# Gate and up projections with two input parts in one matmul, and a PSUM layout to match

## The chip, the cores and the metric

The kernel runs on one core of a Trainium2 chip. The metric is the device time of one execution in microseconds (us). TensorE (PE) multiplies, VectorE (DVE) and ScalarE (ACT) work elementwise, GpSimd (POOL) subtracts, SyncE (SP) starts the loads of weights. PSUM is the memory that matmuls write; one bank holds 512 fp32 values per partition.

## The reference, cut to what matters

The program is two transformer stacks in a row on 256 tokens of 1,024 features: two layers of (feed-forward, mixer of four branches, feed-forward), then four layers of (mixer, cross attention, feed-forward). The change is in the eight feed-forward stages:

```python
def _swiglu(x, w_gate, w_up, w_down):
    return (jax.nn.silu(x @ w_gate) * (x @ w_up)) @ w_down
# in each layer, D = 1024, D_FF = 2816 everywhere:
x = x + 0.5 * _swiglu(_rmsnorm(x, norm), w_gate, w_up, w_down)   # first stack
x = x + _swiglu(rmsnorm(x, norm), w_gate, w_up, w_down)          # second stack
```

## The kernel before

All weights are cut into 460 units of 1 MB (128 partitions x 2,048 fp32 values), used in a fixed order. Five slots hold them (`RING = 5`). For each unit SP loads `raw` once the unit five places earlier is done (L382 to L386), ACT makes the high part `wh` by rounding to the short fp32r form (L1113), and POOL makes the low part `wl = raw - wh` (L400). POOL takes over from unit 2; DVE makes the low parts of the first two (L1768, L1800).

Activations are kept features by tokens, also as a high and a low part (`ah`, `al` for the input of a stage, `gh`, `gl` for the gated values). A product of a weight tile of 128x128 with 256 tokens is three matmuls into the same 256 columns of a bank, each with its own load of the stationary tile (`product`, L451 to L457):

```python
pe.matmul(out, sl, vh, ...)   # L454  low weights  x high input
pe.matmul(out, sh, vl, ...)   # L455  high weights x low input
pe.matmul(out, sh, vh, ...)   # L456  high weights x high input
```

A unit is 16 such products, 48 matmuls of 256 columns. A feed-forward stage (`ffn`) has 22 units of gate and up in turn (0 gate, 1 up, 2 gate, and so on), each 2x256 columns in one bank of the ring G0 to G3, and then 11 units of `down` that accumulate in the four banks of S0 and S1. So gate and up are 176 units in the program, 2,816 products, 8,448 of the 24,180 matmuls.

The norm's factor per token (`root`, used through the view `along`) is not applied to the input but to the result in PSUM. It is ready only after unit 1, since the row sums are matmuls put halfway into and behind unit 1 (`row_sums_apart`, L560). For each pair of units DVE does five operations of 128x512 (`pair`, L1914 to L1929): scale the gate (L1919), scale the up value (L1921), multiply with ACT's silu (L1924), round to `gh` (L1927), subtract to `gl` (L1929). ACT does the silu between the first two and the third (L1269), and in its program order each silu stands behind the rounding of the unit four places ahead. PE takes a bank of G again when silu (for a gate unit) or the subtraction (for an up unit) four units earlier has passed.

Around a feed-forward stage stands this order. Its input arrives in PSUM: in the four G banks after a mixer, in S0 and S1 after another feed-forward stage, which happens once (end of layer 0 to begin of layer 1 in the first stack). DVE adds the residual (L1872, L1959), cuts the low part (L1776) and copies the sum to SBUF (L1783, signal `x_kept`); only then is the PSUM tile free.

In the first feed-forward stage the kernel also makes position tables: PE computes them behind unit 2 (L1077), DVE copies them (L1936), and ACT starts 12 DMAs (`send_tables`, L1683), one after each pair 1 to 8 and two after pairs 9 and 10. DVE waits for all 12 before the first mixer (L2753).

Of the kernel before, what the change touches and what calls it, by code (L numbers as in the profile page):

```python
# [128 lines left out]
def build(nc, w_units, params_d, consts_d, hot_d, rel_d, x_d, mem_d, ws_d, bs_d, out_d,  # L129
# [14 lines left out]
    wl = sb("wl", RING * UW, F32R, offset=at[0] - 4 * RING * UW)  # L144
    wh = sb("wh", RING * UW, F32R)
# [3 lines left out]
    ah = sb("ah", KD * T, F32R)  # L149
    al = sb("al", KD * T, F32R)  # L150
    full = sb("full", KD * T)
    mh = sb("mh", KD * T, F32R)
    ml = sb("ml", KD * T, F32R)
# [18 lines left out]
    gh = w("gh", 0, FP * 512, F32R)  # L172
    gl = w("gl", FP * 512, FP * 512, F32R)
# [17 lines left out]
    oh, ol = w("oh", 0, 2048, F32R), w("ol", 2048, 2048, F32R)  # L191
# [17 lines left out]
    hoh, hol = w("hoh", 4096, 2048, F32R), w("hol", 8192, 2048, F32R)  # L209
# [6 lines left out]
    soh, sol = w("soh", 8192, 2048, F32R), w("sol", 10240, 2048, F32R)  # L216
# [18 lines left out]
    G = [nc.alloc_psum_tensor(f"G{i}", [P, 512], F32) for i in range(4)]  # L235
    S = [nc.alloc_psum_tensor(f"S{i}", [P, 1024], F32) for i in range(2)]
# [126 lines left out]
    with nc.Block() as block:  # L363
# [49 lines left out]
        def _(pe):  # L413
# [4 lines left out]
            gfree, sfree = {}, {}  # L418
            also = {}

            def bank(ring, nxt, free, by, signals=1):

                k = nxt[0]
                nxt[0] += 1
                if k - len(ring) in free:
                    pe.wait_ge(*free[k - len(ring)])
                expect[by.name] = expect.get(by.name, 0) + signals
                free[k] = (by, expect[by.name])
                return ring[k % len(ring)]

            def g_bank(by):
                return bank(G, gbank, gfree, by)

            def s_bank(by, signals=1):
                if sbank[0] - len(S) in also:
                    pe.wait_ge(*also[sbank[0] - len(S)])
                return bank(S, sbank, sfree, by, signals)

            def g_bank_until(by, count):

                k = gbank[0]
                gbank[0] += 1
                if k - len(G) in gfree:
                    pe.wait_ge(*gfree[k - len(G)])
                gfree[k] = (by, count)
                return G[k % len(G)]

# [3 lines left out]
            def product(out, parts, start, stop, **kw):  # L451

                for k, (sh, sl, vh, vl) in enumerate(parts):
# [5 lines left out]
            def features(out, j, xh, xl, fcs=2, col=256, halfway=None):  # L459

                for fc in range(fcs):
                    if fc and halfway is not None:
                        halfway()
                    for k in range(KD):
                        parts = [(wcut(wh, j, k * 256 + fc * P, P), wcut(wl, j, k * 256 + fc * P, P),
                                  xh[:, k * T:(k + 1) * T], xl[:, k * T:(k + 1) * T])]
# [3 lines left out]
            def features_by_input(out, j, xh, xl, acts, pieces=False):  # L470

                for k in range(KD):
# [4 lines left out]
                    for fc in range(2):  # L477
                        parts = [(wcut(wh, j, k * 256 + fc * P, P), wcut(wl, j, k * 256 + fc * P, P),
                                  xh[:, k * T:(k + 1) * T], xl[:, k * T:(k + 1) * T])]
# [4 lines left out]
            def tokens_by_input(out, j, xh, xl, acts):  # L484

                for k in range(KD):
                    if k % 2 == 0:
                        pe.wait_ge(acts, c.next(acts))
                    for tb in range(TB):
                        a = k * T + tb * P  # L490
                        parts = [(xh[:, a:a + P], xl[:, a:a + P], wcut(wh, j, k * 256, 256), wcut(wl, j, k * 256, 256))]
# [4 lines left out]
            def tokens(out, j, xh, xl, first=0, width=256, base=0):  # L496

                for tb in range(TB):
                    parts = [(xh[:, k * T + tb * P:k * T + tb * P + P], xl[:, k * T + tb * P:k * T + tb * P + P],
                              wcut(wh, j, k * 256 + first, width), wcut(wl, j, k * 256 + first, width))  # L500
                             for k in range(KD)]
# [3 lines left out]
            def projection(count, by, xh, xl, acts=None, kind="features"):  # L505
                for u in range(count):
# [4 lines left out]
                    if kind == "features" and first is not None:  # L511
                        ins = features_by_input(out, j, xh, xl, first)
                    elif kind == "features":
                        ins = features(out, j, xh, xl)
                    elif first is not None:
                        ins = tokens_by_input(out, j, xh, xl, first)
                    else:
                        ins = tokens(out, j, xh, xl)
                    ins.then_inc(unit_done, 1)
                    unit[0] += 1  # L520

# [53 lines left out]
            def ffn(memory=False):  # L575
# [3 lines left out]
                g0 = gbank[0]  # L579

                def unit_of(j, u, n, free):
                    if free is not None:
                        pe.wait_ge(*free)
                    if n:
                        pe.wait_ge(low_ready, n + 1)
                    if u == 1:
                        part = row_sums_apart()
                    if u == 0:
                        ins = features_by_input(G[g0 % 4], n0 % RING, ah, al, acts_ready, pieces=n == 0)
                    else:  # L590
                        halfway = (lambda: part(0)) if u == 1 else None
                        if memory and u == 13:
                            sums = norm_sums_apart(memn)
                            halfway = lambda: sums(0, KD // 2)
                        ins = features(G[(g0 + j) % 4], (n0 + j) % RING, ah, al, halfway=halfway)
# [2305 lines left out]
```

## Time and profile before

| what | value |
|---|---|
| median of 3 runs | 2871.94 us |
| lowest and highest run | 2865.34 and 2881.08 us |
| profiled execution, first to last instruction (span) | 2878.8 us |
| PE busy | 2822.3 us, 98% |
| POOL, ACT, DVE busy | 73%, 46%, 37% |
| granted TensorE clock, mean | 0.989 |

The profile gives the profiled execution's span; no time of its own is listed beside it. It lies inside the three runs, 0.24% above their median. Durations of single matmuls (some 280 ns) contain the length of the pipeline; how fast matmuls follow each other is seen from the time of many divided by their number.

### The profile page before, as it was taken

How to read it: one execution, taken by the hardware profiler on the slowest of the kernel's cores; microseconds unless marked ns; L12 is line 12 of the kernel's file. 1: busy time of each engine (PE TensorE's matmuls, PEld its weight loads, DVE VectorE, ACT ScalarE, POOL GpSimd, SP SyncE). 2: the span in 40 equal slices, each digit the busy share in tenths (PEclk: the TensorE clock that was granted, in tenths of full speed). 3: DMA queues.
4: the chain of work that ended last, by engine and by line, in shares of the span. 5: the costliest groups of instructions: out<-in, count | busy, mean ns of one | idle time of the engine just before them, and what ended most of it. 6: DMA issues, size and time to landing. Idle time of an engine off the chain costs nothing.

```text
span 2878.8 us, 55910 instructions
## 1 busy us (share of the span) xinstructions
PE 2822.3 (98%) x24180; PEld 2771.7 (96%) x24180; DVE 1066.5 (37%) x1865; ACT 1333.4 (46%) x1490; POOL 2108.9 (73%) x462
## 2 busy tenths in 40 slices
PE   8999999999999999999999999999999999999998
PEld 8999889999999899999999998999999999999998
DVE  4217534213155443445333144333123331453331
ACT  5335544344355454345443484444354443454442
POOL 6777657878876578776768783659886688767785
PEclk9999999999999899999999999999999999999999
DMA  7974344555554355554445542445554455544553
GB/s 231 193 198 170 135 144 176 191 185 188 199 184 152 112 192 189 182 185 147 168 169 191 191 177 87 158 144 197 191 204 153 147 195 196 191 147 161 176 192 116
DMA packets 74197, 496.88 MB, mean 173 GB/s; under 512 B 8399, under 2 KB 13135, under 8 KB 14968
## 3 DMA queue, kind: packets, MB, share of 16 engines
q1 hardware_dynamic: 68344, 485.88, 46.9%
q10 hardware_dynamic: 5632, 7.62, 2.7%
q8 instruction: 191, 3.13, 0.4%
q14 instruction: 30, 0.25, 0.0%
HBM read 490.05 MB, written 3.41 MB: 171 GB/s over the span
## 4 chain that ended last, share of the span: by engine, by line
PE 86%; POOL 4%; DMA 3%; issue 3%; DVE 2%; ACT 2%; ACTq 0%; SPq 0%; POOLq 0%; DVEq 0%
PE G L454 21%; PE G L456 21%; PE G L455 21%; PE S L454 5%; PE S L456 5%; PE S L455 5%; POOL wl L400 4%; DMA raw<-w_units 2%; PE G L691 1%; PE S L1042 1%; ACT wh L1113 1%; DMA bias<-tables 0%; PE S L842 0%; PE S L799 0%; PE S L805 0%
## 5 line engine op out<-in xcount | busy, mean ns | idle before, releaser
L400 POOL TENSOR_TENSOR wl<-raw,wh 128x2048 fp32r<-128x2048 f32 x458 | 2108.7, 4616 | 740.5 <-ACT wh L1113 719.0
L1113 ACT ACTIVATE wh<-raw 128x2048 fp32r<-128x2048 f32 x456 | 873.7, 1918 | 1045.6 <-DMA raw<-w_units 1045.5
L454 PE MATMUL G<-ah,wl 128*128 128x256 f32 x4304 | 1209.2, 281 | 15.6 <-DVE wl L1768 8.9
L455 PE MATMUL G<-al,wh 128*128 128x256 f32 x4304 | 1200.6, 279 | 0.0
L456 PE MATMUL G<-ah,wh 128*128 128x256 f32 x4304 | 1200.3, 279 | 0.0
L454 PEld LDWEIGHTS G<-ah,wl 128*128 128x128 f32 x4304 | 816.4, 190 | 24.1 <-issue 15.1
L455 PEld LDWEIGHTS G<-al,wh 128*128 128x128 f32 x4304 | 815.2, 189 | 0.6
L456 PEld LDWEIGHTS G<-ah,wh 128*128 128x128 f32 x4304 | 814.1, 189 | 0.0
L454 PE MATMUL S<-gh,wl 128*128 128x256 f32 x1408 | 391.4, 278 | 3.4 <-POOL wl L400 3.4
L455 PE MATMUL S<-gl,wh 128*128 128x256 f32 x1408 | 391.3, 278 | 0.0
L456 PE MATMUL S<-gh,wh 128*128 128x256 f32 x1408 | 391.2, 278 | 0.0
L454 PEld LDWEIGHTS S<-gh,wl 128*128 128x128 f32 x1408 | 265.0, 188 | 3.7 <-issue 3.7
L456 PEld LDWEIGHTS S<-gh,wh 128*128 128x128 f32 x1408 | 265.1, 188 | 0.0
L455 PEld LDWEIGHTS S<-gl,wh 128*128 128x128 f32 x1408 | 265.1, 188 | 0.0
L1921 DVE TENSOR_TENSOR G<-G,root 128x512 f32<-128x512 f32 x88 | 61.5, 698 | 361.3 <-PE G L456 361.3
L1959 DVE SCALAR_TENSOR_TENSOR S<-S,x 128x512 f32<-128x512 f32 x28 | 19.6, 700 | 367.1 <-PE S L456 365.9
L1919 DVE TENSOR_TENSOR G<-G,root 128x512 f32<-128x512 f32 x88 | 61.4, 698 | 184.4 <-PE G L456 184.1
L454 PE MATMUL G<-mh,wl 128*128 128x256 f32 x384 | 108.3, 282 | 3.3 <-DVE ml L2120 2.8
L454 PE MATMUL G<-wh,al 128*128 128x256 f32 x384 | 108.0, 281 | 0.8 <-DVE ll L2563 0.8
L455 PE MATMUL G<-wl,ah 128*128 128x256 f32 x384 | 107.2, 279 | 0.0
L456 PE MATMUL G<-wh,ah 128*128 128x256 f32 x384 | 107.1, 279 | 0.0
L456 PE MATMUL G<-mh,wh 128*128 128x256 f32 x384 | 106.9, 279 | 0.0
(371 smaller groups left out, 3786.3 us busy)
## 6 DMA issues: line engine op xcount, KB each, us to landing
raw<-w_units SPq DMA_DIRECT2D x459, 1024.0 KB, 4.8
bias<-tables ACTq DMA_DIRECT2D x24, 128.0 KB, 3.2
tables<-trow ACTq DMA_DIRECT2D x12, 192.0 KB, 9.0
con<-consts SPq DMA_DIRECT2D x1, 1056.0 KB, 16.8
x<-x_in SPq DMA_DIRECT2D x4, 256.0 KB, 5.8
raw<-w_units SPq DMA_DIRECT2D x4, 256.0 KB, 6.9
memx<-mem_in ACTq DMA_DIRECT2D x1, 1024.0 KB, 7.4
out<-full SPq DMA_DIRECT2D x4, 256.0 KB, 2.5
```

The costliest lines, as they stand in the source:

```text
L400: pool.tensor_tensor(wl[:, j * UW:(j + 1) * UW], raw[:, j * UW:(j + 1) * UW], wh[:, j * UW:(j + 1) * UW].bitcast(F32), ALU.subtract)\
L454: pe.matmul(out, sl, vh, start=start and k == 0, stop=False, **kw)
L455: pe.matmul(out, sh, vl, start=False, stop=False, **kw)
L456: ins = pe.matmul(out, sh, vh, start=False, stop=stop and k == len(parts) - 1, **kw)
L691: ins = pe.matmul(out, v_of(kc), pt[:, kc * 512 + n * P:kc * 512 + (n + 1) * P], start=kc == 0, stop=kc == nk // P - 1)
L1042: ins = pe.matmul(out[:, h * T:(h + 1) * T], qf[:, f * T + g * P:f * T + (g + 1) * P], kc[:, f * T:(f + 1) * T], start=dc == 0, stop=dc == 1)
L1113: act.activation(wh[:, j * UW:(j + 1) * UW], raw[:, j * UW:(j + 1) * UW], ACT.Copy)\
L1919: dve.tensor_tensor(pairs(gate), pairs(gate), along, ALU.mult).then_inc(scaled, 1)
L1921: dve.tensor_tensor(pairs(value), pairs(value), along, ALU.mult).then_inc(up_scaled, 1)
L1959: dve.scalar_tensor_tensor(xs if last else held[k], held[k], factor, xs, ALU.mult, ALU.add)\
```

## The change

Three things change.

- Gate and up units use `slot_product`: a matmul with the high weights streams high and low input, 512 columns, into two slots of 256 in one bank, and a matmul with the low weights adds low weights x high input to the first slot. That is two matmuls and two loads for a product. The pairs of SBUF tensors become one tensor each, at the same addresses, so that one access pattern reaches both parts.
- A unit now fills two banks. Units take the four tiles of two banks (G01, G23, S0, S1) by a list, `unit_tiles`. Ordinary stages go round four tiles, starting with an S tile; the first stage and the one that also prepares the memory input go round three after unit 3.
- DVE scales both slots and adds them: three operations of 512 columns for each unit in place of one.

The tables move: their matmuls stand behind unit 5, the copy behind pair 2, and ACT starts two DMAs after each of the pairs 4 to 9. The residual units after a mixer start at an even G bank. All other products, the 88 `down` units among them, remain three matmuls.

```diff
+            def slot_product(bank, parts, start, stop):
+                two = bank.rearrange("p (s n) -> p s n", s=2)
+                for k, (sh, sl, vh, vl, both) in enumerate(parts):
+                    pe.matmul(two, sh, both, start=start and k == 0, stop=False, skip_group_check=True)
+                    ins = pe.matmul(two[:, 0, :], sl, vh, start=False, stop=stop and k == len(parts) - 1,
+                                    skip_group_check=True)
+                return ins
...
+            def slot_features(tile, j, xs, halfway=None):
+                for fc in range(2):
+                    if fc and halfway is not None:
+                        halfway()
+                    parts = [weights_still(j, k * 256 + fc * P, xs, k * T) for k in range(KD)]
+                    ins = slot_product(tile[:, fc * 512:(fc + 1) * 512], parts, True, True)
+                return ins
...
+    def unit_tiles(gbank, sbank, first, memory):
+        held, sums, other = [(gbank // 2 + n) % 2 for n in range(2)], 2 + sbank % 2, 2 + (sbank + 1) % 2
+        assert gbank % 2 == 0
+        if first or memory:
+            start = held + [other, sums] if first else [other] + held + [sums]
+            rest = [(held + [sums])[(u - 4) % 3] for u in range(4, 2 * FP - 1)]
+            return start + rest + held[0:1]
+        return [([other] + held + [sums])[u % 4] for u in range(2 * FP)]
...
# DVE, for each unit
+                def scale_slots(tile, spare):
+                    total, other = slots(tile)
+                    spare = pairs(full[:, spare * 512:(spare + 1) * 512])
+                    dve.tensor_tensor(spare, other, along, ALU.mult).then_inc(vec_step, c.one(vec_step))
+                    dve.tensor_tensor(total, total, along, ALU.mult).then_inc(vec_step, c.one(vec_step))
+                    dve.wait_ge(vec_step, c.sofar(vec_step))
+                    return total, dve.tensor_tensor(total, total, spare, ALU.add)
...
-                    dve.tensor_tensor(pairs(gate), pairs(gate), along, ALU.mult).then_inc(scaled, 1)
+                    scale_slots(Q[tiles[u - 1]], 2)[1].then_inc(scaled, 1)
...
# PE, for each unit u of tile t
+                    claim([2 * t, 2 * t + 1], (gated_ready, v0 + u // 2 + 1) if u % 2 else (silu_ready, s0 + u // 2 + 1))
...
# ACT
             def send_tables(p):
-                if p == 1:
+                if p == 4:
                     act.wait_ge(trow_ready, 2)
-                heads = {9: (8, 9), 10: (10, 11)}.get(p, (p - 1,)) if p else ()
+                heads = range(2 * p - 8, 2 * p - 6) if 4 <= p < 10 else ()
```

## Rows read from the trace of the kernel before

**Rows 1.** The page: busy time by engine, and the chain by engine.

```profile
PE 2822.3 (98%) x24180; PEld 2771.7 (96%) x24180; DVE 1066.5 (37%) x1865; ACT 1333.4 (46%) x1490; POOL 2108.9 (73%) x462
PE 86%; POOL 4%; DMA 3%; issue 3%; DVE 2%; ACT 2%; ACTq 0%; SPq 0%; POOLq 0%; DVEq 0%
```

**Rows 2.** Stretches (from:to length, busy time and count by engine, clock, DMA share, GB/s).

```profile
463.00:576.00 113.00, 113.00 (x960) 112.94 (x960) 38.64 (x56) 45.68 (x35) 92.32 (x21) 1.00 0.53 187
651.00:760.00 109.00, 109.00 (x962) 108.94 (x961) 38.64 (x56) 45.84 (x35) 93.34 (x21) 1.00 0.54 194
760.00:820.00 60.00, 60.00 (x532) 60.00 (x531) 7.26 (x13) 23.18 (x17) 51.22 (x12) 1.00 0.51 177
1141.00:1186.00 45.00, 45.00 (x382) 44.92 (x381) 26.22 (x36) 18.82 (x16) 34.29 (x8) 1.00 0.53 188
1187.00:1248.00 61.00, 61.00 (x521) 61.00 (x520) 8.32 (x14) 23.30 (x17) 49.95 (x12) 1.00 0.49 173
```

**Rows 3.** Pieces of the chain: start, length, what, count.

```profile
1412.63 6.91 PE S L1042 x32
```

**Rows 4.** Timeline of PE: start, length, what, count.

```profile
831.70 0.95 PE L549 MATMUL S<-ones,full 128*128 128x1 f32 x8
832.58 0.38 PE L725 MATMUL S<-x,sp 128*4 128x256 f32 x1
...
1475.75 0.59 PE L560 MATMUL S<-full,ones 128*128 128x256 f32 x2
1476.00 0.47 PE L454 MATMUL G<-ah,wl 128*128 128x256 f32 x1
1476.30 0.28 PE L455 MATMUL G<-al,wh 128*128 128x256 f32 x1
```

**Rows 5.** Groups by line: mean ns of one behind the busy time.

```profile
L400 POOL TENSOR_TENSOR wl<-raw,wh 128x2048 fp32r<-128x2048 f32 x458 | 2108.7, 4616 | 740.5 <-ACT wh L1113 719.0
L1921 DVE TENSOR_TENSOR G<-G,root 128x512 f32<-128x512 f32 x88 | 61.5, 698 | 361.3 <-PE G L456 361.3
```

**Rows 6.** Timeline of DVE, second and third stage with feed-forward.

```profile
467.54 0.70 DVE L1919 TENSOR_TENSOR G<-G,root 128x512 f32<-128x512 f32 x1
...
486.06 0.70 DVE L1921 TENSOR_TENSOR G<-G,root 128x512 f32<-128x512 f32 x1 [4.95 <-PE G L456]
...
641.11 1.28 DVE L1783 COPY x<-S 128x512 f32<-128x512 f32 x2
```

**Rows 7.** Timeline of PE where feed-forward follows feed-forward.

```profile
638.39 0.28 PE L456 MATMUL S<-gh,wh 128*128 128x256 f32 x1
638.50 0.28 PE L454 MATMUL G<-ah,wl 128*128 128x256 f32 x1
```

**Rows 8.** DMA from 50 to 200 us: queues (packets, MB, share), issues.

```profile
q1 hardware_dynamic: 3829, 27.86, 46.9%
q10 hardware_dynamic: 1584, 2.16, 38.0%
raw<-w_units SPq DMA_DIRECT2D x26, 1024.0 KB, 8.7
tables<-trow ACTq DMA_DIRECT2D x11, 192.0 KB, 9.0
```

**Rows 9.** First stage: stretches as in rows 2, and PE's wait.

```profile
100.00:140.00 40.00, 40.00 (x342) 40.00 (x341) 12.29 (x18) 14.86 (x10) 30.23 (x8) 1.00 0.93 218
140.00:180.00 40.00, 37.68 (x320) 37.50 (x320) 2.78 (x4) 13.89 (x8) 27.69 (x7) 1.00 0.94 212
PE S L454 <- POOL wl L400: 3.4, 2, 2.3
```

**Rows 10.** Timeline of ACT: arrivals of weights beside doubled tables.

```profile
149.99 1.31 ACTq L1683 DMA_DIRECT2D tables<-trow  x2
155.53 1.92 ACT L1113 ACTIVATE wh<-raw 128x2048 fp32r<-128x2048 f32 x1 [3.64 <-DMA raw<-w_units]
173.03 1.92 ACT L1113 ACTIVATE wh<-raw 128x2048 fp32r<-128x2048 f32 x1 [8.72 <-DMA raw<-w_units]
```

More of the change, by code:

```diff
@@ L417, in _, with claim, expected, g_bank_until @@
             expect = {}
[L418 to L426, printed above, removed]
-                expect[by.name] = expect.get(by.name, 0) + signals
-                free[k] = (by, expect[by.name])
-                return ring[k % len(ring)]
-            def g_bank(by):
[L432 to L446, printed above, removed]
+            busy = {}
+            def claim(banks, *until):
+                asked = []
+                for b in banks:
+                    asked += [w for w in busy.get(b, ()) if w not in asked]
+                    busy[b] = until
+                for w in asked:
+                    pe.wait_ge(*w)
+            def expected(by, signals=1):
+                expect[by.name] = expect.get(by.name, 0) + signals
+                return by, expect[by.name]
+            def g_bank_until(by, count):
+                b = gbank[0] % len(G)
+                gbank[0] += 1
+                claim([b], (by, count))
+                return G[b]
+            def g_bank(by):
+                return g_bank_until(*expected(by))
+            def s_bank(by, signals=1, *also):
+                k = sbank[0] % len(S)
+                sbank[0] += 1
+                claim([4 + 2 * k, 5 + 2 * k], expected(by, signals), *also)
+                return S[k]
+            inputs, memory, gated_in = (ahl, KD * T), (mhl, KD * T), (ghl, FP * 512)
+            heads, hgrn_heads, sgu_out = (ohl, KD * T), (hohl, 2 * KD * T), (sohl, KD * T)
             def wcut(t, j, first, width):
@@ L578, in ffn, with one @@
                 s0, v0 = expect.get("silu_ready", 0), c.taken.get("gated_ready", 0)
[L579 to L583, printed above, removed]
+                tiles = unit_tiles(gbank[0], sbank[0], n0 == 0, memory)
+                def one(u):
+                    n, t = n0 + u, tiles[u]
+                    claim([2 * t, 2 * t + 1], (gated_ready, v0 + u // 2 + 1) if u % 2 else (silu_ready, s0 + u // 2 + 1))
                     if n:
                         pe.wait_ge(low_ready, n + 1)
[L586 removed]
+                    if u == 0:
+                        ins = slot_features_by_input(Q[t], n % RING, inputs, acts_ready, pieces=n == 0)
+                    elif u == 1:
                         part = row_sums_apart()
[L588 to L595 removed]
+                        ins = slot_features(Q[t], n % RING, inputs, lambda: part(0))
+                    elif memory and u == 13:
+                        sums = norm_sums_apart(memn)
+                        ins = slot_features(Q[t], n % RING, inputs, lambda: sums(0, KD // 2))
+                    else:
+                        ins = slot_features(Q[t], n % RING, inputs)
                     ins.then_inc(unit_done, 1)
@@ L600, in unit_of @@
                         sums(KD // 2, KD)
+                        c.next(acts_ready, KD // 2)
+                    if n0 == 0 and u == 5:
+                        claim([6, 7], (trow_ready, 2))
+                        bias_tables()
                 for u in range(2 * FP):
-                    if u < 4:
-                        free = gfree.get(g0 + u - 4)
-                    else:
-                        free = (silu_ready, s0 + u // 2 - 1) if u % 2 == 0 else (gated_ready, v0 + u // 2 - 1)
-                    unit_of(u, u, n0 + u, free)
-                    if n0 == 0 and u == 2:
-                        bias_tables()
-                    if memory and u == 13:
-                        c.next(acts_ready, KD // 2)
+                    one(u)
                 unit[0] += 2 * FP
-                gbank[0] += 2 * FP
                 expect["silu_ready"] = s0 + FP
-                for k in range(4):
-                    u = 2 * FP - 4 + k
-                    gfree[gbank[0] - 4 + k] = ((silu_ready, s0 + u // 2 + 1) if u % 2 == 0
-                                               else (gated_ready, v0 + u // 2 + 1))
                 n1 = unit[0]
-                if not n0:
-                    pe.wait_ge(trow_ready, 2)
                 y = [s_bank(x_kept, 2), s_bank(x_kept, 2)]
```

211 lines of the change are left out of this document (116 added, 95 removed).

## The prediction

> **What bounds the kernel now.** I read the page first: busy time by engine and the chain by engine. PE is busy 98% of the span and is 86% of the chain; POOL is at 73%, DVE at 37% [rows 1]. So only what shortens PE's own stream pays, as long as nothing else becomes late. Then I read stretches, because the mean duration of a matmul (some 280 ns) is not its pace. In the gate and up part of the second feed-forward stage (463 to 576 us) 960 matmuls take 113.0 us, 117.7 ns each. In the third (651 to 760 us) 962 take 109.0 us, 113.3 ns each [rows 2]. The granted clock is 1.00 in both, the 2.4 GHz level, at which 256 columns are 106.7 ns. So a matmul of 256 columns costs 7 to 11 ns more than its columns, and there are two paces. They hold for long stretches and change between them: `down` runs at 112.8 ns in 760 to 820 us and at 117.1 in 1187 to 1248 us; the last gate and up units of the fourth stage (1141 to 1186 us) run at 117.8 [rows 2]. I call them quick and slow. The four last feed-forward stages read as the third. Counted over the program, some 62 of the 176 gate and up units are slow: 22 of the first stage, 22 of the second, 9 of the fourth, and the first one or two of the others, behind the row sums. 114 are quick.
>
> What makes the extra? Two kinds of rows. Eight matmuls of one column, each with a load of a 128x128 tile, start 0.88 us apart in all (831.70 to 832.58), 110 ns each [rows 4]: that is the price of a load with next to nothing to stream. And 32 matmuls of 256 columns in plain fp32 take 6.91 us, 216 ns each [rows 3]: they stream for 213 ns, and a load for each adds only 3. So a load of about 110 ns is hidden whole behind a stream of 213 ns, and is itself the limit, with a few ns of hand-over, behind one of 107 ns. That is what the change can win: of three loads for a product one goes, one hides behind 512 columns, and one still stands behind 256.
>
> **The product.** Before: 3 x 117.7 = 353 ns slow, 3 x 113.3 = 340 ns quick. After: the 512 columns at 216 ns, by the fp32 row that streams as long, and a 256-column matmul behind it. The nearest row for the second is the place where the stream goes from fp32 to fp32r: from the first of two sum matmuls at 1475.75 to L455 at 1476.30 are 0.55 us, less 2 x 0.216 leaves 118 ns for the L454 between [rows 4]. With the quick pace it would be 113. So 329 to 334 ns; I take 332, since the nearest row is on the slow side. The bounds: all loads hidden, columns alone, 768 at 2.4 GHz = 320 ns and two hand-overs of 3 ns make 326; and a cost that goes by columns, 3 x 113.3 = 340 ns.
> By 332: slow units 62 x 16 x 21 ns = 20.8 us, quick units 114 x 16 x 8 ns = 14.6 us. **Term 1: -35.4 us** (at 326 -52.3; at 340 -12.9).
>
> The trace shows a load at 110 ns and a matmul pace of 113 or 118 [rows 2, 4]. The Trainium skill, "TensorE: Matmul & The Clock Gate", section "Back-to-back issue gap", gives for a warm matmul N/2.4 + 2.5 ns, with the next load drawn ahead beside it. By that rule 256 columns cost 109.2 ns and a product 327.5 ns before and 325 after: the change would win 2.5 ns a product, 7 us in all. The trace speaks against its value for before (340 to 353) and agrees on the long stream (216 for 213); if its 325 held for after, term 1 would be about -55 us. The page's section "LDWEIGHTS (loading the stationary operand)" has 107 ns for 128 columns, and the row of one-column matmuls (110) is near it.
>
> **DVE and ACT.** Each unit gets two more operations of 128x512. The scaling took 698 ns [rows 5]; multiply to SBUF and add I put at the same. A pair then has 9 operations, 6.3 us and some waits, in a period of 2 x 16 x 0.332 = 10.6 us. DVE idles 4.95 us in front of the second scaling [rows 6], so there is room: it is hidden by PE's next unit. The gate's tile is free 2.1 + 0.6 us after its unit, the up tile 6 x 0.7 = 4.3 us after; with four tiles PE comes back three units later (15.9 us), with three tiles two units later (10.6 us). At the start of a stage the norm's factor comes late: the first scaling in the second stage begins at 467.54 [rows 6], when units 0 and 1 are done. Then silu is past at 470.3 and the up tile at 474; the first reuses come at about 473 and 478. Hidden. In the fourth stage unit 4 takes the tile of unit 1 (the list starts `other, G01, G23, sums` and goes on with G01), which is about 0 to 1 us late, once: 0.5 us. POOL needs 4.62 us for a unit [rows 5], PE will need 5.31: the supply still holds.
>
> **Where feed-forward follows feed-forward.** There the stage's input lies in S0 and S1, and unit 0 wrote to a free G bank: PE goes from `down` to unit 0 without a gap, 638.39 to 638.50 [rows 7]. After, unit 0 wants the S tile `other`, which is the second of these two. It is free when DVE's last copy to x has ended: 641.11 + 1.28 = 642.4 [rows 6], 3.9 us later. Nothing hides it, apart from 0.5 us that PE waits later for the row sums. **Term 2: +3.4 us**, once. After a mixer the S tile is free and the G banks are copied before unit 1: nothing.
>
> **The first stage and its tables.** Between 100 and 180 us the DMA engines are 93 and 94% busy [rows 9]. The tables hold 38.0% of 16 engines for 11 of them in 150 us, 5.2 us of all engines each; 26 units hold 46.9%, 2.7 us each [rows 8]. One table in each pair of units is 5.2 + 5.4 = 10.6 us of DMA in a pair of 11.3: it just fits. Two in a pair, as the change sends them from pair 4 to pair 9, are 15.8 us in a pair of 10.6. The trace shows what two do: after four tables at 137.7 and 150.0 ACT's next arrivals stand at 155.53, 162.39 and 173.03, with 8.72 us of idle time for the last [rows 10], and PE waits 3.4 us for POOL, in two waits [rows 9]. For twelve: the queue of tables lasts some 62/0.55 = 113 us from about 75 us on; the weights get 51 us of it, 19 units where PE wants 21. Two units are 11 us. Part of that the ring takes: with five slots the weights of a unit can be asked for four units early (21 us), of which landing (8.7 us [rows 8]), ACT and POOL (1.9 and 4.6) use 15, so 6 us are left. That makes a stall of 5 us, on top of one like the 3.4 us of now, which comes from the same cause; with the doubt in the sharing 3 to 12 us in place of 3.4. **Term 3: +5 us** (bounds -2, the early tables no longer delaying anything, and +20, if weights get only 40% of the DMA, as after 137.7 us). All tables land before some 190 us, ahead of the first mixer at 205: DVE's wait for them is hidden, but has only 15 us of cover.
>
> **The pace behind it.** `down` and the mixers are not touched, but pace is inherited from what ran before. If `down` turned quick in all three slow stages it would give 3 x 528 x 4.4 ns = 7 us, if slow in all five quick ones cost 11.6 us. I put nothing, and keep -7 and +12 for the range.
>
> **Sum.** -35.4 + 0.5 + 3.4 + 5 = -26.5 us on the span of 2878.8, which becomes 2852. The span is 0.24% above the median of the runs; the same step from 2871.9 gives **2845 us**, 0.9% less.
>
> **Rivals.**
> 1. Every load hides (326 ns). For it: the 216 ns of the fp32 rows, two passes with a load. Against: no 256-column fp32r stretch is under 113. Term 1 is -52.3, the time 2829. (The Trainium skill's rule above, from the section "Back-to-back issue gap", would end here too.)
> 2. Cost goes by columns, 340 ns: then the extra is in reading fp32r, not in the load. For it: quick pace and columns give the same ratio whatever is loaded. Against: the load at 110 ns alone. Term 1 is -12.9, the rest +9: 2868, no change to be seen.
> 3. Tables starve the first stage (+20 in place of +5): 2860. For it [rows 10]; against: the ring's lead had held with one table a pair.
> 4. Other side: the long stream leaves PE in the slow pace, and it lasts. Behind sums that stream 213 ns the pace was the slow one in the row I used. Of the matmuls outside gate and up 15,700 remain, some 8,200 of them now quick: 5 x 528 in `down` and, my estimate from the starts in the trace, 60% of the mixers' 9,400 fp32r ones. At 4.4 ns they cost 36 us, and the product 334, 5 us more: 2845 + 41 = 2886. It is slower than before from about 5,100 turned matmuls on. Against: the pace turned quick again within two units in six of the eight stages.
> 5. The change does not do what it says, if the DVE chain holds the tiles: it would show as waits on `gated_ready`; the 4.3 us against 10.6 leave it under 2 in 100, and I give it no case.
>
> **How the numbers follow.** Forecast 0.45 (its own range 2832 to 2857), rival 1 0.20, rival 2 0.16, rival 3 0.10, rival 4 0.09. What can be told from no change is 0.5%, 14 us: under 2857.6 is faster, over 2886.3 slower. Faster: 0.43 + 0.20 + 0.04 of rivals 2 and 3 = 0.67. Slower: rival 4 ends at the border; with mishaps beside it 0.07. Same: 0.26. The range goes from 2814 (rival 1 with quick `down`) to 2868, which cuts rival 4 and half of rival 2.
>
> **What would show it.** Between 1480 and 1590 us two matmuls take 332 ns together, and a unit 5.31 us in place of 5.44; 326 or 340 ns tell for rivals 1 and 2. At the one change from feed-forward to feed-forward PE's first wait is on DVE's copy, some 4 us. In the first stage PE waits for POOL between 120 and 190 us, 5 to 12 us in all. DVE's busy time grows by 176 x 2 x 0.7 = 246 us. Behind the last gate and up unit `down` stands at 113 or 118 ns. I am wrong if PE waits elsewhere in the gate and up units, or if a product is outside 326 to 340.

## The result and the profile after

The changed kernel takes 2931.04 us (median of 4 runs, 2928.02 to 2932.41), the kernel before 2875.26 us beside it (2865.34 to 2881.08). The ratio is 1.019, with a 95% interval of 1.017 to 1.022: it is slower by 56 us. I had forecast 2845 us and a range of 2814 to 2868, so even the sign is wrong. Of the two profiled executions the spans are 2929.0 and 2878.8 us, 50 us apart, at the same mean clock of 0.989.

The page of the changed kernel: busy time by engine, the groups of the slot products' two matmuls into the G tiles (L487 with 512 columns, L488 with 256; the S tiles have 1,280 more of each), and the landing time of the tables (issue count, KB, us):

```profile
span 2929.0 us, 50637 instructions
PE 2860.1 (98%) x21364; PEld 2678.1 (91%) x21364; DVE 1294.3 (44%) x2217; ACT 1339.2 (46%) x1490; POOL 2110.2 (72%) x462
...
L487 PE MATMUL G<-ahl,wlh 128*128 128x512 f32 x1536 | 555.8, 403 | 24.3 <-DVE wlh L1822 10.1
...
L488 PE MATMUL G<-ahl,wlh 128*128 128x256 f32 x1536 | 434.6, 283 | 0.0
...
tables<-trow ACTq DMA_DIRECT2D x12, 192.0 KB, 16.1
```

PE executes 2,816 matmuls fewer than in [rows 1] and is busy 38 us longer; it stays the bound. DVE gains 228 us of work and still has room. The timeline of PE in the second gate and up part (start, length, what):

```profile
520.10 0.28 PE L488 MATMUL G<-ahl,wlh 128*128 128x256 f32 x1
520.22 0.40 PE L487 MATMUL G<-ahl,wlh 128*128 128x512 f32 x1
520.45 0.28 PE L488 MATMUL G<-ahl,wlh 128*128 128x256 f32 x1
520.57 0.40 PE L487 MATMUL G<-ahl,wlh 128*128 128x512 f32 x1
```

From one start of L487 to the next are 0.35 us: 0.23 to 0.24 for the 512 columns, 0.12 for the 256. Stretches (from:to length, busy time and count of PE, loads, DVE, ACT, POOL, clock, DMA share, GB/s) give it more closely; the first two rows are gate and up of the second and `down` of the third feed-forward stage, the next two gate and up and `down` of the fifth:

```profile
480.00:580.00 100.00, 100.00 (x568) 86.86 (x568) 58.59 (x88) 42.12 (x29) 84.95 (x19) 1.00 0.53 188
782.00:842.00 60.00, 60.00 (x512) 60.00 (x512) 6.87 (x12) 21.18 (x16) 49.66 (x11) 1.00 0.49 175
1502.00:1602.00 100.00, 100.00 (x568) 86.82 (x567) 59.72 (x89) 41.99 (x31) 81.50 (x19) 1.00 0.53 187
1616.00:1676.00 60.00, 60.00 (x512) 60.00 (x511) 6.72 (x12) 21.20 (x15) 48.80 (x11) 1.00 0.50 176
```

568 matmuls in 100 us are 284 products of 352 to 353 ns, in every stage. That is the slow pace of before (353) and 13 ns more than the quick one (340, [rows 2]). `down`, untouched by the change, runs at 117.2 ns in both stretches, where it had 112.8 [rows 2].

The ends of the units in both traces divide the span. In us, for each part; "whole" is a gate and up part with its `down`:

| part | before | after | difference |
|---|---|---|---|
| 1st feed-forward, gate and up / down | 143.5 / 66.0 | 159.3 / 62.2 | +12.0 whole |
| 2nd | 125.2 / 62.2 | 125.2 / 62.2 | 0.0 |
| 3rd (behind the 2nd) | 121.6 / 59.8 | 130.9 / 62.2 | +9.2, +2.3 |
| 4th (memory) | 126.0 / 62.2 | 128.6 / 62.2 | +2.7 |
| 5th to 8th, each | 120.7 / 59.8 | 125.2 / 62.2 | +4.5, +2.3 |
| mixers and attention, six | 1376.7 | 1373.0 | -3.7 |

So: 26 us is pace in gate and up (4 x 4.5, 5.2 in the third once its wait is taken off, 2.7 in the fourth), 12 is pace in five `down` parts, some 4 a wait in the third stage, 12 the first stage, less 4 in the mixers.

The wait in the third stage stands in the timelines of PE and DVE of the changed kernel:

```profile
649.42 0.28 PE L480 MATMUL S<-ghl,wlh 128*128 128x256 f32 x1
653.57 0.66 PE L487 MATMUL S<-ahl,wlh 128*128 128x512 f32 x1 [3.87 <-DVE x L1837]
```
```profile
652.24 1.28 DVE L1837 COPY x<-S 128x512 f32<-128x512 f32 x2
```

In the first stage PE no longer waits for POOL but for tiles, because ACT's silu stands behind a late rounding. ACT's timeline, then PE's with the two longest waits and the DVE operation behind the second, and two stretches around these waits:

```profile
100.70 7.88 ACTq L1737 DMA_DIRECT2D tables<-trow  x2
119.04 1.91 ACT L1167 ACTIVATE wlh<-raw 128x2048 fp32r<-128x2048 f32 x1 [16.42 <-DMA raw<-w_units]
120.86 0.58 ACT L1324 ACTIVATE full<-G 128x512 f32<-128x512 f32 x1
...
147.09 1.91 ACT L1167 ACTIVATE wlh<-raw 128x2048 fp32r<-128x2048 f32 x1 [16.44 <-DMA raw<-w_units]
148.91 0.58 ACT L1324 ACTIVATE full<-S 128x512 f32<-128x512 f32 x1
```
```profile
116.95 0.28 PE L488 MATMUL G<-ahl,wlh 128*128 128x256 f32 x1
121.49 0.79 PE L487 MATMUL G<-ahl,wlh 128*128 128x512 f32 x1 [4.27 <-ACT full L1324]
...
151.79 0.80 PE L487 MATMUL G<-ahl,wlh 128*128 128x512 f32 x1 [6.00 <-DVE ghl L1994]
```
```profile
149.59 0.70 DVE L1989 TENSOR_TENSOR G<-full,G 128x512 f32<-128x512 f32 x1 [7.38 <-ACT full L1324]
```
```profile
116.00:124.00 8.00, 3.73 (x15) 2.94 (x14) 2.39 (x4) 2.70 (x3) 2.97 (x1) 0.83 0.92 284
145.00:156.00 11.00, 5.00 (x20) 4.07 (x19) 3.98 (x6) 6.24 (x5) 6.92 (x2) 0.69 0.98 278
```

ACT stands idle 16.4 us for the weights of a unit. Its silu comes behind their rounding and frees PE's tile at 121.4. The second time the silu comes at 148.91, DVE has waited 7.38 us for it, and PE's tile is an up tile, which is free only after DVE's subtraction. Behind both waits PE goes on with the clock at its lower level: the granted clock of the two stretches is 0.83 and 0.69, and slot products take 0.64 us for some 3 us each time. The start of a pair of tables held ACT's queue for 7.88 us from 100.70, but that ended at 108.6, ten us before these weights had landed, so this wait of PE is the weights' and not the issue's.

### The profile page after: what moved, and what is told of

Same layout as the page of the kernel before. It is cut to its first block, busy times and chain, and to the rows that moved or that the text cites. A ratio compares the mean times of both kernels' runs of the same rounds, so it can differ in the third digit from the quotient of the medians.

```text
span 2929.0 us, 50637 instructions
## 1 busy us (share of the span) xinstructions
PE 2860.1 (98%) x21364; PEld 2678.1 (91%) x21364; DVE 1294.3 (44%) x2217; ACT 1339.2 (46%) x1490; POOL 2110.2 (72%) x462
## 4 chain that ended last, share of the span: by engine, by line
PE 89%; DMA 5%; DVE 2%; ACT 2%; issue 1%; SPq 0%; ACTq 0%; DVEq 0%
PE G L487 12%; PE G L478 11%; PE G L480 11%; PE G L479 11%; PE S L487 10%; PE G L488 6%; PE S L479 6%; PE S L480 6%; PE S L478 6%; PE S L488 5%; DMA raw<-w_units 5%; PE G L749 1%; PE S L1096 1%; ACT wlh L1167 1%; DMA bias<-tables 0%
## 5 line engine op out<-in xcount | busy, mean ns | idle before, releaser
L420 POOL TENSOR_TENSOR wlh<-raw,wlh 128x2048 fp32r<-128x2048 f32 x458 | 2110.0, 4619 | 788.1 <-ACT wlh L1167 765.1
L1167 ACT ACTIVATE wlh<-raw 128x2048 fp32r<-128x2048 f32 x456 | 873.0, 1917 | 1008.4 <-DMA raw<-w_units 1008.0
L487 PE MATMUL G<-ahl,wlh 128*128 128x512 f32 x1536 | 555.8, 403 | 24.3 <-DVE wlh L1822 10.1
L487 PE MATMUL S<-ahl,wlh 128*128 128x512 f32 x1280 | 456.2, 399 | 3.9 <-DVE x L1837 3.9
L488 PE MATMUL G<-ahl,wlh 128*128 128x256 f32 x1536 | 434.6, 283 | 0.0
L478 PE MATMUL G<-ahl,wlh 128*128 128x256 f32 x1488 | 422.1, 284 | 2.1 <-DVE merged L2243 2.1
L479 PE MATMUL G<-ahl,wlh 128*128 128x256 f32 x1488 | 417.4, 280 | 0.0
L480 PE MATMUL G<-ahl,wlh 128*128 128x256 f32 x1488 | 417.2, 280 | 0.0
L480 PE MATMUL S<-ghl,wlh 128*128 128x256 f32 x1408 | 395.6, 281 | 0.0
L479 PE MATMUL S<-ghl,wlh 128*128 128x256 f32 x1408 | 395.6, 281 | 0.0
L478 PE MATMUL S<-ghl,wlh 128*128 128x256 f32 x1408 | 395.6, 281 | 0.0
L487 PEld LDWEIGHTS G<-ahl,wlh 128*128 128x128 f32 x1536 | 292.1, 190 | 97.1 <-issue 10.0
L488 PE MATMUL S<-ahl,wlh 128*128 128x256 f32 x1280 | 360.4, 282 | 0.0
L487 PEld LDWEIGHTS S<-ahl,wlh 128*128 128x128 f32 x1280 | 241.3, 189 | 64.0 <-DVE x L1837 4.1
L478 PEld LDWEIGHTS G<-ahl,wlh 128*128 128x128 f32 x1488 | 284.8, 191 | 8.8 <-issue 5.3
L488 PEld LDWEIGHTS G<-ahl,wlh 128*128 128x128 f32 x1536 | 291.9, 190 | 0.4
L479 PEld LDWEIGHTS G<-ahl,wlh 128*128 128x128 f32 x1488 | 283.1, 190 | 0.2
L480 PEld LDWEIGHTS G<-ahl,wlh 128*128 128x128 f32 x1488 | 283.1, 190 | 0.0
L478 PEld LDWEIGHTS S<-ghl,wlh 128*128 128x128 f32 x1408 | 270.3, 192 | 0.4
L479 PEld LDWEIGHTS S<-ghl,wlh 128*128 128x128 f32 x1408 | 264.3, 188 | 0.0
L480 PEld LDWEIGHTS S<-ghl,wlh 128*128 128x128 f32 x1408 | 264.3, 188 | 0.0
L488 PEld LDWEIGHTS S<-ahl,wlh 128*128 128x128 f32 x1280 | 241.1, 188 | 0.0
```

The source lines that it names most:

```text
L420: pool.tensor_tensor(wl[:, j * UW:(j + 1) * UW], raw[:, j * UW:(j + 1) * UW], wh[:, j * UW:(j + 1) * UW].bitcast(F32), ALU.subtract)\
L487: pe.matmul(two, sh, both, start=start and k == 0, stop=False, skip_group_check=True)
L488: ins = pe.matmul(two[:, 0, :], sl, vh, start=False, stop=stop and k == len(parts) - 1, skip_group_check=True)
L1167: act.activation(wh[:, j * UW:(j + 1) * UW], raw[:, j * UW:(j + 1) * UW], ACT.Copy)\
```

## The experiments

Two theories stood after this. **A:** an fp32r matmul costs by its streamed columns, whatever is loaded, and "quick" is something that only a stream of 256-column matmuls has; the long matmul cannot be quick and leaves slow pace behind. **Rivals:** the two pieces of the 512 columns cost (B); the load beside the stream costs (C); DVE's additions or the two-slot tiles disturb PE (R).

**A bench of TensorE alone (m1_paces).** The core of its edit:

```diff
+            for i in range(N):
+                pe.matmul(out()[:, 0:512], st(i), mv(i, 512), start=True, stop=True)     # L94
...
+            for i in range(N):
+                pe.matmul(out()[:, 0:512].rearrange("p (s n) -> p s n", s=2), st(i), two[:, :, i % 7 * T:i % 7 * T + 256],     # L97
+                          start=True, stop=True)
...
+            for i in range(N):
+                pe.matmul(out()[0:32, 0:512], st(i, 32), mv(i, 512), start=True, stop=True)     # L113
```

Expected:

> A bench of TensorE alone (it leaves the whole computation out and returns the input): after 64 warming matmuls, sections of 48 matmuls, each its own source line, with full 128x128 stationary tiles in turn. The first six follow six plain fp32 matmuls each: fp32r with 256 columns, 512 columns in one piece, 512 in two pieces 8 KB apart (as the changed kernel streams them), 384 columns, and 512 and 256 in turn; then 256 with full and with 32-column stationary tiles, 512 with 32-column ones, 256 columns with the moving address shifted by 0, 64, 128 and 192 bytes, bf16 with 256 and 512 columns, fp32 with 256. Theory A (cost goes by streamed fp32r column, 0.44 to 0.46 ns each, whatever is loaded): 512 columns take 227 to 235 ns in one piece and in two, 384 take 170 to 176, and 32-column tiles change nothing. Theory B (the two pieces cost): 512 in one piece take 216 ns, in two 235. Theory C (the load beside the stream slows the stream or is the limit): with 32-column stationary tiles 256 columns fall to about 109 ns and 512 to 216, with full ones 235 in one piece too.

Timeline of PE in the bench (start, length of the section, line, count); the shape in front is contraction by stationary columns:

```profile
30.03 5.81 PE L91 MATMUL b<-a,w 128*128 128x256 f32 x48
38.07 11.55 PE L94 MATMUL b<-a,w 128*128 128x512 f32 x48
51.86 11.55 PE L97 MATMUL b<-a,w 128*128 128x512 f32 x48
65.66 8.73 PE L101 MATMUL b<-a,w 128*128 128x384 f32 x48
101.83 5.60 PE L111 MATMUL b<-a,w 128*32 128x256 f32 x48
107.27 11.25 PE L113 MATMUL b<-a,w 128*32 128x512 f32 x48
118.36 5.61 PE L115 MATMUL b<-a,w 128*128 128x256 f32 x48
123.80 5.90 PE L117 MATMUL b<-a,w 128*128 128x256 f32 x48
129.54 5.82 PE L119 MATMUL b<-a,w 128*128 128x256 f32 x48
140.89 5.41 PE L123 MATMUL b<-ab,wb 128*128 128x256 bf16 x48
146.36 10.31 PE L125 MATMUL b<-ab,wb 128*128 128x512 bf16 x47
156.50 20.88 PE L127 MATMUL b<-x,raw 128*128 128x256 f32 x96
```

From start to start inside the sections: 512 fp32r columns 233.3 ns in one piece (L94) and 233.3 in two (L97), 384 columns 174.6, 256 columns 113.3 (the first few gaps of a section are left out). With 32-column stationary tiles 256 and 512 columns take 113.3 and 231.1. So B and C fall. bf16 takes 109.2 and 215.8 ns. Plain fp32 with 256 columns shows 215.8 ns a record, and 96 records for the 48 matmuls of the code: one such matmul takes 432 ns, in two records. The row on which I had built (216 ns) is such a record of plain fp32; fp32r at 512 columns costs 17 ns more. 512 and 256 in turn (L105, L106) take 235 and 118 ns, the changed kernel's numbers, with no other engine at work. With the moving address shifted by 64 bytes, 256 columns take 119.9 ns, right behind a section at 113.3: the address bears on the pace too. The sections shifted by 128 and 192 bytes take 117.8 and 118.7 ns, but they came behind the slow one, so this bench does not tell whether their address or what ran before them made them slow.

For this the Trainium skill, "TensorE: Matmul & The Clock Gate", section "Back-to-back issue gap", has N/2.4 + 2.5 ns for the gap of an isolated warm matmul; the estimate by it is 109.2 and 215.8 ns for 256 and 512 columns. The bf16 rows of the bench agree to the tenth; the fp32r rows, with 113.3 to 117.8 and 233.3, do not.

**The old three matmuls in the new layout (e_three).**

```diff
-                    pe.matmul(two, sh, both, start=start and k == 0, stop=False, skip_group_check=True)
-                    ins = pe.matmul(two[:, 0, :], sl, vh, start=False, stop=stop and k == len(parts) - 1,
-                                    skip_group_check=True)
+                    pe.matmul(two[:, 0, :], sl, vh, start=start and k == 0, stop=False, skip_group_check=True)
+                    pe.matmul(two[:, 1, :], sh, vl, start=False, stop=False, skip_group_check=True)
+                    ins = pe.matmul(two[:, 0, :], sh, vh, start=False, stop=stop and k == len(parts) - 1,
+                                    skip_group_check=True)
```

> The changed kernel with the old three matmuls of 256 columns in a slot product (low weights x high input and high weights x high input in slot 0, high weights x low input in slot 1); tiles, DVE's additions and tables stay as changed. Theory A or C (the 512-column stream runs at the slow pace and leaves PE in it): a product goes back to 340 ns in the four last gate and up stages, down to 113 ns, and the stage pairs (gate and up, down) to 120.7 and 59.8 us: 4 x 4.5 + 5 x 2.3 + 4.5 for the third stage, about 30 to 34 us faster than the changed kernel, so about 2898 us, still 20 above the kernel before for the tables and the tile wait. Theory R (it is DVE's extra operations or the slots, by PSUM accesses beside PE's writes, that slow PE): the pace stays 118 ns and the time 2930 us.

Measured: 2884.48 us, 1.003 of before (1.001 to 1.006). Its stretches in the fifth stage, gate and up, then `down`:

```profile
1476.00:1576.00 100.00, 100.00 (x880) 99.89 (x879) 59.98 (x91) 44.31 (x33) 85.33 (x19) 1.00 0.54 191
1590.00:1650.00 60.00, 60.00 (x532) 60.00 (x531) 7.75 (x13) 22.66 (x16) 50.89 (x12) 1.00 0.49 176
```

880 matmuls in 100 us are 113.6 ns, 341 a product, beside the same DVE work (59.98 us in 100). R falls. Taking the long matmul away is worth 46 us by the medians. Not all of it is loss against the kernel before: 7 of it is the second stage, slow before and after, which turned quick here (120.7 and 59.8). That, and a first stage of 213.8 us in place of 221.5, is why it did better than the 2898 that I expected. The fourth stage stayed as in the changed kernel (128.6 and 62.2), so its 2.7 us are not shown to be the long matmul's.

**Two places undone (e_places).**

```diff
-                heads = range(2 * p - 8, 2 * p - 6) if 4 <= p < 10 else ()
+                heads = {3: (0,), 4: (1,), 5: (2,), 6: (3,), 7: (4, 5), 8: (6, 7), 9: (8, 9), 10: (10, 11)}.get(p, ())
...
-        return [([other] + held + [sums])[u % 4] for u in range(2 * FP)]
+        ring = held + [other, sums] if chained else [other] + held + [sums]
+        return [ring[u % 4] for u in range(2 * FP)]
```

> The changed kernel with two places undone as far as its layout allows: tables go out one for each of the pairs 3 to 6 and two for each of 7 to 10, in place of two for each of 4 to 9; and where feed-forward follows feed-forward the ring of tiles starts with the two G tiles, so that unit 0 need not wait for the S tile. Both theories of the two places: the first stage's gate and up part falls from 159.3 us toward 148 (tables) and the third's from 130.9 to about 127 (the 4.2 us wait before unit 0 gone); in all 11 to 16 us faster than the changed kernel, 2915 to 2920. Rival for the first stage (three tiles in turn and silu behind a late rounding hold PE, not the tables): it stays above 156 us.

Measured: 2916.02 us, 1.014 of before (1.009 to 1.019), 15 us under the changed kernel. The third gate and up part falls from 130.9 to 125.9 us: the wait, 3.9 us in the trace, is gone. The first stage's falls from 159.3 to 143.7, but its `down` rises from 62.2 to 69.5, since the last four tables have still to land; PE then waits there once for POOL:

```profile
PE S L479 <- POOL wlh L421: 4.8, 1, 4.8
```

The stage as a whole gains 8 us. The rival, three tiles in turn as the cause by themselves, falls: by it gate and up would have stayed above 156 us. What is left of it is that the tiles pass on the lateness of weights.

**All three places together (e_both_c).** The edits of the last two in one kernel.

> The changed kernel with three matmuls of 256 columns in a slot product, the tables spread over pairs 3 to 10 and the G tiles first where feed-forward follows feed-forward; DVE's two more operations a unit and the two-slot tiles stay. If these three places are the whole loss, it is level with the kernel before within 0.3%, gate and up at 120.7 us in the ordinary stages: 2870 to 2882. If DVE's additions or the slots cost something that the other runs hid, it stays 10 us or more above before.

Measured: 2879.19 us, 1.001 of before (0.999 to 1.003). The gate and up parts of the fifth stage and of those behind it take 120.7 us and their `down` parts 59.8, as in the kernel before, beside 61.93 us of DVE's work in 100:

```profile
1480.00:1580.00 100.00, 100.00 (x885) 100.00 (x884) 61.93 (x94) 42.08 (x29) 85.92 (x19) 1.00 0.54 196
```

So there DVE's additions cost nothing, and the three places account for the loss. The level time of the whole is in part a matter of luck, though: the second stage turned quick (7 us less than before) and the mixers take 5 us less, while the first stage takes 7 us more than before (148.5 and 68.2 us), with eight of the tables still going out in pairs and one long wait of PE:

```profile
PE G L488 <- DVE ghl L1996: 7.9, 1, 7.9
```

How much of the first stage's 7 us is the tables' and how much the three tiles' or the additions' is not shown.

**What pace is inherited (m2_inherit, m3_nudge).** The sections of the first bench with the unshifted address had been quick. The second bench runs units of 48 matmuls in the kernel's order behind different things:

```diff
+            slots(2)
+            triple(1)
+            plain(2)
+            triple(1)
+            plain(8)
+            triple(1)
+            half(1)
+            triple(1)
```

> A second bench of TensorE alone (the computation is left out and the input returned), with the kernel's own order: units of 48 matmuls of 256 columns (low weights x high input, high weights x low input, high weights x high input, 8 deep into one bank half), and between them: slot products as changed, plain fp32 matmuls (2, then 8), one or two bf16 ones, a single fp32 of 128 columns, and fp32r matmuls that always stream the high input. Theory A1 (two paces of a 256-column stream by the phase in which it was entered): units behind slot products and behind plain matmuls run at 118 ns as in the whole kernel, units behind a bf16 matmul or after single ones can be at 113. Theory A2 (the slow pace needs what is not in the bench: traffic of the other engines or of the DMAs, or waits at unit borders): all units run at 113.3 ns.

Timeline of PE in this bench; L81 is a unit, L95 the end of the slot products, L100 plain fp32 (two records a matmul), L105 bf16:

```profile
47.37 0.28 PE L95 MATMUL b<-a,w 128*128 128x256 f32 x1
47.49 5.82 PE L81 MATMUL b<-a,w 128*128 128x256 f32 x48
53.14 1.02 PE L100 MATMUL b<-x,raw 128*128 128x256 f32 x4
53.81 5.82 PE L81 MATMUL b<-a,w 128*128 128x256 f32 x48
59.47 3.61 PE L100 MATMUL b<-x,raw 128*128 128x256 f32 x16
62.73 6.00 PE L81 MATMUL b<-a,w 128*128 128x256 f32 x48
68.58 0.28 PE L105 MATMUL b<-ab,wb 128*128 128x256 bf16 x1
68.62 5.71 PE L81 MATMUL b<-a,w 128*128 128x256 f32 x48
```

Once a unit has set in, it runs at 117.8 ns behind slot products (5.82 us), at 113.3 behind two plain ones (its first gap is longer), at 117.8 behind eight, and at 113.3 behind one bf16 matmul (5.71). The same 48 matmuls on the same SBUF addresses have two paces, with no DMA and no other engine at work: the pace depends on what ran before. The PSUM bank changes from unit to unit, but the unit behind slot products (slow) and the one behind a bf16 matmul of 128 columns (quick) write the same one. A2 falls. A unit behind two bf16 matmuls, or behind one plain one of 128 columns, was slow.

The third bench asks whether one bf16 matmul, a nudge, does it always.

```diff
+            slots(1)
+            half(1)
+            triple(1)
+            half(1)
+            triple(1)
+            plain(8)
+            half(1)
+            triple(1)
```

> A third bench of TensorE alone (computation left out, input returned): one bf16 matmul of 256 columns ahead of a unit of 48 fp32r matmuls of 256 columns, behind slot products, behind 8, 4 and 2 plain fp32 matmuls, and behind a quick unit; also three bf16 ones, one of 128 columns, one plain one; and slot products behind a bf16 one. Theory A1 (a pace by phase of entry, which one bf16 matmul sets to the quick one): units right behind a single bf16 matmul run at 113.3 ns each time, and slot products keep 235 + 118 and leave slow pace behind them. Theory A3 (the nudge only shifts the phase by one step, so what follows depends on what was before): behind slots or 8 plain ones it is quick, behind others slow.

```profile
35.95 0.28 PE L105 MATMUL b<-ab,wb 128*128 128x256 bf16 x1
35.99 5.70 PE L81 MATMUL b<-a,w 128*128 128x256 f32 x48
...
44.35 0.28 PE L105 MATMUL b<-ab,wb 128*128 128x256 bf16 x1
44.40 5.70 PE L81 MATMUL b<-a,w 128*128 128x256 f32 x48
49.94 0.28 PE L105 MATMUL b<-ab,wb 128*128 128x256 bf16 x1
49.98 5.71 PE L81 MATMUL b<-a,w 128*128 128x256 f32 x48
```

Behind fp32r matmuls, quick or slow, one bf16 matmul (five times of 256 columns, twice of 128) was followed by 113.3 ns each time, 7 of 7 in both benches together. Behind plain fp32 it was quick in one case of three (behind two, not behind four or eight), and three bf16 in a row left it slow. Slot products behind a nudge kept 235 and 118 ns. So A1 holds for a nudge between fp32r matmuls. Behind plain fp32 neither theory is right: A3 had quick behind eight plain ones.

**The nudge ahead of `down` in the changed kernel (e_down).**

```diff
+                    if first:
+                        pe.matmul(y[0][:, 0:T], ones[:, 0:HD].bitcast(BF16), ones[:, 0:P].bitcast(BF16),
+                                  start=True, stop=True, skip_group_check=True)
```

> The changed kernel with one more matmul, bf16, 256 columns, into the first bank of `down` ahead of each of the eight `down` parts; its values are overwritten. Theory A1: `down`, which is slow in all eight stages since slot products run before it, turns quick: 62.2 becomes 59.9 us in seven or eight of them, in all 16 to 18 us faster than the changed kernel, about 2914. Rival (slow `down` comes from the S tiles, the tensors joined into one or DVE's traffic): it stays at 62.2 and 2931.

Measured: 2916.35 us, 1.014 of before (1.008 to 1.020), 15 us under the changed kernel. `down` takes 59.9 us in all eight stages. The fifth:

```profile
1617.00:1657.00 40.00, 40.00 (x355) 40.00 (x354) 0.00 (x0) 13.45 (x7) 34.11 (x8) 1.00 0.54 201
```

355 in 40 us, 112.7 ns, one line of code away from the 117.2 of the changed kernel. So the slow pace of `down` does not come from its tiles, its tensors or DVE's traffic, but from what PE ran before it.

**The nudge in the kernel before (e_nudge, e_nudge2_c).** First ahead of unit 2, directly behind the row sums, and ahead of the next projection behind sums and scores:

```diff
+                        if u == 2 or memory and u == 14:
+                            nudge(G[(g0 + j) % 4], True)
```

> The kernel before with such a bf16 matmul where its trace turned slow: ahead of unit 2 of each gate and up part (and of unit 14 where the memory's sums stand in unit 13), ahead of `down` in the first stage, and ahead of the next projection unit behind row sums, layer sums and cross attention's scores; the values are overwritten. Theory A1: the slow stretches (some 9,100 matmuls at 117.8 ns) turn to 113.3 for the most part; 20 to 35 us faster than before, about 2845. Theory A3: some quick ones turn slow in exchange, and the time is within 10 us of before.

Measured: 2867.30 us, 0.996 of before (0.993 to 1.000). I had expected 20 to 35 us and it is 10. Of the parts that were slow, the `down` of the fourth stage turned quick (62.2 to 59.8), and gaps of 116 to 120 ns between matmuls fell from 8,559 to 6,236; the second stage stays slow (125.3 and 62.2). There the nudge stood behind plain fp32, where the third bench has it uncertain. Then one unit later and ahead of every `down` (the edit against the first trial):

```diff
-                        if u == 2 or memory and u == 14:
+                        if u == 3 or memory and u == 15 or not n0 and u == 4:
...
-                    if first and not n0:
+                    if first:
```

> The kernel before with the bf16 matmul put one unit later, between two fp32r units (ahead of unit 3, of unit 15 with the memory's sums, of unit 4 in the first stage, ahead of every `down`, and ahead of the second projection unit behind row sums, layer sums and scores). In the benches a single one behind fp32r matmuls was followed by the quick pace each time (7 of 7), one behind plain fp32 not always (1 of 3). Theory A1: the second feed-forward stage turns quick too (125.2 and 62.2 to 121 and 59.9), and more of the mixers; 10 to 25 us under the kernel before. Theory A3: the turned ones are others than planned, and it is no faster than the first trial of this, 0.996 of before.

Measured: 2866.54 us, 0.997 of before (0.996 to 0.999), no faster than the first trial beyond the spread of the runs. All feed-forward stages are quick; the second (the stretch that had 960 matmuls in 113.0 us in [rows 2]):

```profile
470.00:570.00 100.00, 100.00 (x885) 100.00 (x884) 31.29 (x45) 39.86 (x29) 89.87 (x20) 1.00 0.55 194
```

113.0 ns. Gaps of 116 to 120 ns fell from 8,559 to 3,260, which at 4.4 ns each should be 23 us. The profiled span fell by 8.6. The feed-forward stages give 4.4 + 2.2 us in the second and 1.2 + 2.2 in the fourth; the first stage's gate and up gives 4.6, of which its `down`, short of weights, takes back 2.1; the added matmuls take some 0.1 us each. The mixers lose 2 in all, though their gaps of 116 to 120 ns fell from 4,317 to 2,797; that waits for DVE and ACT take up there what the matmuls gain is my reading, which no run tested. I had hoped for 10 to 25 us; it is 7 by the medians, and by the time alone the result is theory A3's. By the trace it is A1 for the feed-forward stages.

## Why the prediction was wrong

- **What bounds the kernel: right.** PE is the bound, and every loss but the first stage's and the one wait in the third is PE's pace.
- **Term 1 failed: "the 512 columns at 216 ns, by the fp32 row that streams as long".** This is the wrong step. I took the extra 7 to 11 ns of an fp32r matmul for a load that is not quite hidden. But it goes with the stream: 512 columns take 233 to 235 ns with a full load beside them, 0.456 to 0.459 ns a column, and 231 with a 32-column one. The row that I carried over (L1042) belongs to another type, whose stream has no such extra (and its 32 records are 16 matmuls of the code). The one-column row [rows 4] was no proof either: it shows that a load costs 110 ns alone, not that it limits. A product became 353 ns, outside 326 to 340, so quick stages lost 4.5 us each and slow ones won nothing. Term 1 is about +26 us in place of -35.
- **Rival 2 had the mechanism,** cost by column, but I priced it at the quick pace (340), though my own rows had a second pace, 3 x 117.7 = 353. With that it would have been a loss. I had let only the better of two rates stand as the bound.
- **The pace behind: "I put nothing" failed,** rival 4 came true in part: all five quick `down` parts turned slow, +12 us, the price that I gave for it. The mixers did not (-4 us): gaps of 116 to 120 ns outside the feed-forward stages are 4,317 before and 4,049 after. I take it that their own sums set the pace anew, but no run shows that. My argument against it, that the pace turned quick again behind sums, does not bear on slot products: behind them it was slow 8 times of 8.
- **Term 2, +3.4 us: right.** The wait is 3.87 us, on the copy that I had named, and e_places takes it away.
- **Term 3, +5 us: right in kind, too small.** It is +12 for the whole stage. Weights come late as reckoned, but PE waits for tiles and not for POOL: twice behind ACT's silu and once, for 6.00 us, behind DVE's subtraction. That is the wait on `gated_ready` of rival 5, put at under 2 in 100, and my own sign of being wrong ("if PE waits elsewhere in the gate and up units"). DVE's chain is not what made it late; it stood idle for a silu behind late weights. And each long wait brings some 3 us at the lower clock, which stood nowhere in the prediction. The upper bound of +20 held the whole.
- **DVE and the fourth stage: right where it can be told.** DVE's new work of 228 us (246 reckoned) is hidden in the ordinary stages, by e_both_c; in the first stage it is not told apart. In the fourth stage PE has no wait.
- **The range** was built from 326 to 340 ns. Its error is the term's: both ends rested on the quick pace. The lower end does not even follow from the terms: rival 1 with quick `down` is 2829 - 7 = 2822 and not 2814.

## What to carry to other kernels

A stream's rate is to be read from rows of the same type: per-column cost of fp32r was not that of plain fp32 passes or of bf16, and fewer loads or fewer, longer matmuls won nothing while loads were hidden. Where a trace shows the same instructions at two rates, price a change at both, and ask what runs ahead of each stretch. Spreading the small-piece DMAs won 8 us in the first stage. And where an engine's program order puts the step that frees a matmul's bank behind the preparation of later weights, late weights stop PE through the bank, before it lacks the weights themselves.

## What the runs showed of the hardware

- fp32r matmuls of 256 columns run at 113.3 or 117.8 ns with the clock at its 2.4 GHz level, on the same addresses, and keep to one for hundreds of matmuls. 384 columns take 174.6, 512 take 233.3 to 235 in one piece or two; bf16 takes 109.2 for 256 columns and 215.8 for 512, and a plain fp32 matmul of 256 columns 432, in two records.
- The quick pace was lost when the moving address was shifted by 64 bytes (119.9 ns). Which mechanism makes the two paces is open; the width of the load is not it (32-column tiles keep 113.3), nor other engines or DMAs (the benches have none at work).
- One bf16 matmul between fp32r ones turned the pace quick 7 times of 7 in the benches, and ahead of `down` 8 times of 8.
- Starting a pair of table DMAs held ACT's queue for 1.1 to 1.9 us in three cases and for 5.18, 7.88 and 8.22 us in three. The two longest came 5 to 6 us behind the start of an earlier pair; what holds the queue is open.
